# The delta rule's chunks of 128 tokens instead of 64, with the state products of one batch between the inverse levels of the next

## The reference

```python
def gated_delta_chunked(q, k, v, g, beta, s0):
    # S_t = a_t (I - b_t k_t k_t^T) S_{t-1} + b_t k_t v_t^T, o_t = S_t^T q_t
    g = jnp.cumsum(g, axis=-1)
    decay = jnp.exp(jnp.where(incl, g[..., :, None] - g[..., None, :], -jnp.inf))
    m = jnp.where(strict, jnp.einsum('bhnid,bhnjd->bhnij', k_beta, k) * decay, 0.0)
    t_inv = lax.linalg.triangular_solve(m + eye, ...)
    u = einsum(t_inv, v * beta)
    w = einsum(t_inv, k_beta * jnp.exp(g))
    def chunk_step(s, xs):
        v_new = u_c - w_c @ s
        o_c = q_c @ s + qk_c @ v_new
        s = s * a_c + k_c^T @ v_new
    ...
o = forward(q, k, v, s_fwd) + flip(backward(...))
```

## Time and profile before

| | us |
|---|---|
| median of 3 runs | 3282.56 (3279.77 to 3286.65) |
| profiled execution: span from first to last instruction | 3284.9 |
| TensorE busy | 2999.6 (91% of the span) |
| VectorE, ScalarE, GpSimd busy | 1235.7, 648.4, 250.2 |
| first block of `delta_net` | 11.85 |
| second block of `delta_net` | 491.7 |

### The profile page before, as it was taken

How to read it: one execution, slowest core, us unless ns; L and a number is a source line. 1 busy time by engine, 2 the same in 40 slices (tenths; PEclk the granted TensorE clock), 3 DMA queues, 4 the chain that set the end, 5 groups by cost and what they waited for, 6 DMA issues and landing times. The chain is left out here.

```text
span 3284.9 us, 43635 instructions
## 1 busy us (share of the span) xinstructions
PE 2999.6 (91%) x18685; PEld 1772.0 (54%) x18685; DVE 1235.7 (38%) x2364; ACT 648.4 (20%) x1444; POOL 250.2 (8%) x347
## 2 busy tenths in 40 slices
PE   6999998999898899999999979799999799999998
PEld 3434663456675555568888864366444444444443
DVE  1052451384443399425555546643001401111111
ACT  2111331011332355122112111532000100000000
POOL 0000110000010000013333310100000000000000
PEclk9999998998879899999999989899999799999999
DMA  7431013240001411000000021301321279999998
GB/s 259 153 133 46 1 52 97 89 78 27 1 1 65 152 52 51 12 29 3 2 2 2 2 88 69 115 1 68 146 76 51 88 322 427 427 427 426 427 427 361
DMA packets 130593, 431.68 MB, mean 131 GB/s; under 512 B 28978, under 2 KB 40502, under 8 KB 102621
## 3 DMA queue, kind: packets, MB, share of 16 engines
q1 hardware_dynamic: 130402, 428.89, 33.7%
HBM read 418.21 MB, written 10.66 MB: 131 GB/s over the span
## 5 line engine op out<-in xcount | busy, mean ns | idle before, releaser
L333 PE MATMUL banks<-weight_ring,rows_turned 128*128 128x512 f32 (+1 forms) x1576 | 679.7, 592 | 34.5 <-DMA weight_ring<-in_w_in 16.6
L333 PEld LDWEIGHTS banks<-weight_ring,rows_turned 128*128 128x128 f32 x1576 | 300.2, 196 | 406.7 <-issue 391.5
L2411 PE MATMUL banks<-rows_turned,weight_ring 128*128 128x256 f32 (+1 forms) x768 | 253.5, 490 | 1.8 <-PEq L1364 1.5
L2411 PEld LDWEIGHTS banks<-rows_turned,weight_ring 128*128 128x128 f32 x768 | 147.6, 192 | 101.0 <-issue 85.9
L3664 PE MATMUL banks<-weight_ring,chosen_turned 128*64 128x512 f32 (+1 forms) x696 | 174.3, 558 | 10.0 <-DMA weight_ring<-in_w_up 6.5
L3664 PE MATMUL banks<-expert_weights_early,chosen_turned 128*64 128x512 f32 (+1 forms) x672 | 169.3, 558 | 11.0 <-DMA expert_weights_early<-in_w_up 7.4
L1432 PE MATMUL banks<-weight_ring,mix_turned 128*128 128x512 f32 x320 | 138.8, 594 | 3.9 <-DMA weight_ring<-in_l_w_out 2.2
L3766 DVE TENSOR_TENSOR hidden<-hidden,banks 128x512 f32<-128x512 f32 (+1 forms) x24 | 14.0, 638 | 324.4 <-PE banks L3664 324.4
L2684 PE MATMUL banks<-v_channels 64*64 64x64 f32 (+1 forms) x2880 | 120.6, 231 | 0.7
L2684 PE MATMUL banks<-weight_ring 64*64 64x64 f32 (+1 forms) x2880 | 115.7, 226 | 0.4
L3664 PEld LDWEIGHTS banks<-weight_ring,chosen_turned 128*64 128x64 f32 x696 | 62.5, 137 | 97.4 <-issue 93.8
(11 more groups left out here) (550 smaller groups left out, 4378.3 us busy)
## 6 DMA issues: line engine op xcount, KB each, us to landing
weight_ring<-in_w_gate SPq DMA_DIRECT2D x29, 1408.0 KB, 17.6
weight_ring<-in_w_up SPq DMA_DIRECT2D x29, 1408.0 KB, 15.1
expert_weights_early<-in_w_gate SPq DMA_DIRECT2D x28, 1408.0 KB, 18.9
expert_weights_early<-in_w_up SPq DMA_DIRECT2D x28, 1408.0 KB, 15.6
expert_weights_early<-in_w_down SPq DMA_DIRECT2D x36, 1024.0 KB, 17.3
weight_ring<-in_w_down SPq DMA_DIRECT2D x35, 1024.0 KB, 17.4
weight_ring<-in_l_w_in SPq DMA_DIRECT2D x15, 2048.0 KB, 8.5
weight_ring<-in_w_in SPq DMA_DIRECT2D x13, 2048.0 KB, 7.8
```

The costliest lines, as they stand in the source:

```text
L333: ins = kit.nc.tensor.matmul(self.bank(u), lhsT, rhs, start=(k == 0), stop=(k == nk - 1))
L2411: ins = nc.tensor.matmul(kit.ps[:, bank(u), 0:n], w[:, k, f * P:(f + 1) * P], hT[:, k, h0:h0 + n], start=(k == 0), stop=(k == KD - 1))
```

## The change

A chunk is now a whole tile of 128 tokens. There are no u and w: the state is multiplied with the keys (`seen`), VectorE forms the residual `beta v - beta exp(g) k S` (`residual`), and the inverse with its decays folded in (`solver`, 128x128) turns it into v_new (`solve`); then `outer` for the state and `output`, which adds queries times state and scores times v_new in PSUM. The inverse keeps its two diagonal 64-blocks by the same levels; the block off the diagonal is two more products (`off`, `cross`). The inverse of the two halves is held with halves swapped, so that `level` and one product of `update` use the two quadrants off the array's diagonal, and the other product of `update` the diagonal ones. Keys are turned to token rows once, in the preparation, in twelve more groups. The decay differences no longer come from a product: the rows of cumulative decays and of their exponentials are parked in DRAM, and SP loads them on all partitions for each batch, 256 KB a load. The decays are not in the matrix while it is inverted, before or after.

The constants (line 1241) and the preparation:

```diff
     for d, before in (("f", col < row), ("b", col > row)):
-        incl = same & (before | (row == col))
-        parts["tri_" + d] = (incl.T) * 1.0
-        parts["tri_half_" + d] = own_half((incl.T) * 1.0)
-        parts["decay_t_" + d] = own_half(np.where(incl.T, 0.0, -NEG))
+        seen = (before | (row == col)).T
+        parts["tri_" + d] = (same & seen) * 1.0
+        parts["unseen_" + d] = np.where(seen, 0.0, -NEG)
     parts["same"] = same * 1.0
-    parts["half0"] = (row < CHUNK) * np.ones((1, P))
-    parts["half1"] = (row >= CHUNK) * np.ones((1, P))
+    parts["other"] = (~same) * 1.0
...
+        groups = list(v_groups)
+        for t in range(TA):
+            for h0 in (0, 4):
+                groups.append(([qk[:, 8 + h, at(t):at(t) + P] for h in range(h0, h0 + 4)], k_tok[:, t, h0 * P:(h0 + 4) * P].rearrange("p (h d) -> p h d", h=4)))
+        G = len(groups)
...
-            for i in range(8):
+            for i in range(10):
                 turn_v(pe, i)
             pe.wait_ge(asked.sem, asked(2))
...
-            for b, name in ((1, "same"), (2, "half0"), (3, "half1")):
-                ins = nc.tensor.matmul(kit.ps[:, b, 0:W], kit.part(name), flat(g), start=True, stop=True)
-            ins.then_inc(summed.sem, 1)
-            for i in range(8, G):
+            nc.tensor.matmul(kit.ps[:, 1, 0:W], kit.part("same"), flat(g), start=True, stop=True)
+            nc.tensor.matmul(kit.ps[:, 1, W:2 * W], kit.part("other"), flat(g), start=True, stop=True)
+            pe.wait_ge(given.sem, given(1))
+            nc.tensor.matmul(kit.ps[:, 0, W:2 * W], kit.part("swap_pairs"), flat(beta), start=True, stop=True).then_inc(summed.sem, 1)
+            for i in range(10, 17):
+                turn_v(pe, i)
+            pe.wait_ge(given.sem, given(3))
+            nc.tensor.transpose(kit.ps[0:W, 2, 0:P], flat(own), kit.ident)
+            nc.tensor.transpose(kit.ps[0:W, 2, P:2 * P], flat(eg), kit.ident).then_inc(summed.sem, 1)
+            for i in range(17, G):
                 turn_v(pe, i)
```

The loads, the products of a level, and TensorE's order:

```diff
+        def sync_loads(sp):
+            sp.wait_ge(parked.sem, parked(32))
+            for b, (r, t) in enumerate(batches):
+                w = (r * TA + t) * H
...
+                        sp.wait_ge(c.solver_ready.sem, c.solver_ready(b))
+                    if outs(b):
+                        sp.wait_ge(c.scores_ready.sem, c.scores_ready(outs(b)))
+                    src = rows_park[0, w + 4 * c.hg:w + 4 * c.hg + 4, :].rearrange("h n -> (h n)")
+                    sp.dma_start(c.decay.rearrange("p h n -> p (h n)"), row_bc(src)).then_inc(c.rows_landed.sem, 16)
+                for c in chains:
+                    if with_out(b):
+                        if outs(b):
+                            sp.wait_ge(c.out_summed.sem, c.out_summed(outs(b)))
+                        src = rows_park[1, w + 4 * c.hg:w + 4 * c.hg + 4, :].rearrange("h n -> (h n)")
+                        sp.dma_start(c.queries.rearrange("p h n -> p (h n)"), row_bc(src)).then_inc(c.queries_landed.sem, 16)
...
+            def level(c, b, i):
...
+                mask = c.odd if i % 2 else c.even
+                for h in range(4):
+                    for o_rows, other in (HALVES, HALVES[::-1]):
...
+            def update(c, b, i):
+                pe.wait_ge(c.z_ready.sem, c.z_ready(6 * b + i + 1))
+                pe.wait_ge(c.inverse_ready.sem, c.inverse_ready(6 * b + i + 1))
+                if b and i == 0:
+                    pe.wait_ge(c.solver_ready.sem, c.solver_ready(b))
+                first, later = in_order(batches[b][0])
+                for h in range(4):
+                    for o_rows, other in (HALVES, HALVES[::-1]):
+                        turned = nc.tensor.matmul(c.low(0)[other, h, :], c.inverse[o_rows, h, :], c.z[o_rows, h, :], start=True, stop=True, tile_position=(o_rows.start, other.start))
+                    for o_rows in HALVES if i < 4 else (later,):
+                        ins = nc.tensor.matmul(c.low(1)[o_rows, h, :], c.z[o_rows, h, :], c.inverse[o_rows, h, :], start=True, stop=True, tile_position=(o_rows.start, o_rows.start))
+                turned.then_inc(c.dt_summed.sem, 1)
+                ins.then_inc(c.d_summed.sem, 1)
...
+            left, right = chains
+            for it in range(N + 1):
...
+                stating = it > 0
+                for c in chains:
+                    keys(c, it)
+                for i in range(5):
+                    for c in chains:
+                        level(c, it, i)
+                    if stating and i == 0:
+                        seen(left, it - 1)
+                    if stating and i == 2:
+                        solve(right, it - 1)
+                    if stating and i == 3:
+                        outer(left, it - 1)
+                    if stating and i == 4:
+                        outer(right, it - 1)
+                    for c in chains:
+                        update(c, it, i)
+                    if stating and i == 0:
+                        seen(right, it - 1)
+                    if stating and i == 1:
+                        solve(left, it - 1)
+                    if stating and i == 2:
+                        output(left, it - 1)
+                    if stating and i == 3:
+                        output(right, it - 1)
+                for c in chains:
+                    off(c, it)
+                scores(left, it)
+                for c in chains:
+                    cross(c, it)
+                scores(right, it)
```

GpSimd's order and VectorE's; `mask` is a masked level, `base`, `shift`, `values`, `rest_keys` and `queries` are each one or two tensor_tensor operations:

```diff
+            for b in range(N):
+                for i in range(3):
+                    for c in chains:
+                        mask(c, b, i)
+                if b + 1 < N:
+                    for c in chains:
+                        base(c, b + 1)
+                shift(chains[0], b)
+                for c in chains:
+                    mask(c, b, 3)
+                shift(chains[1], b)
+                for c in chains:
+                    mask(c, b, 4)
+                for c in chains:
+                    values(c, b)
+                for c in chains:
+                    rest_keys(c, b)
+                for c in chains:
+                    queries(c, b)
...
+            def matrix(c, b):
+                dve.wait_ge(c.keys_summed.sem, c.keys_summed(b + 1))
+                nc.vector.tensor_tensor(c.matrix, c.high(0), per_row(c, beta, b, CHUNK), ALU.mult).then_inc(c.turned_ready.sem, 1)
+                if b:
+                    dve.wait_ge(c.solver_ready.sem, c.solver_ready(b))
+                dve.wait_ge(c.base_ready.sem, c.base_ready(b + 1))
+                step(dve, nc.vector.tensor_tensor(c.turned, c.high(0), c.base_mask, ALU.mult))
+                nc.vector.tensor_tensor(c.turned, c.turned, over_heads("ident_half"), ALU.add).then_inc(c.turned_ready.sem, 1)
+
+            def inverse_base(c, b):
+                name = f"level_{'fb'[batches[b][0]]}1"
+                dve.wait_ge(c.turned_ready.sem, c.turned_ready(7 * b + 1))
+                for o_rows, other in (HALVES, HALVES[::-1]):
+                    ins = nc.vector.tensor_tensor(c.inverse[other], c.matrix[o_rows], over_heads(name, o_rows), ALU.mult)
+                step(dve, ins)
+                nc.vector.scalar_tensor_tensor(c.inverse, c.inverse, -1.0, over_heads("ident_half"), ALU.mult, ALU.add).then_inc(c.inverse_ready.sem, 1)
...
+            def solver_own(c, b):
...
+                for o_rows in HALVES:
+                    nc.vector.tensor_tensor(c.solver[o_rows, :, o_rows], c.turned[o_rows], c.decay[o_rows, :, o_rows], ALU.mult)
+
+            def solver_off(c, b):
+                first, later = in_order(batches[b][0])
+                dve.wait_ge(c.d_summed.sem, c.d_summed(6 * b + 6))
+                nc.vector.scalar_tensor_tensor(c.solver[first, :, later], c.low(1)[first], -1.0, c.decay[first, :, later], ALU.mult, ALU.mult).then_inc(c.solver_ready.sem, 1)
...
+            def residual(c, s):
...
+                dve.wait_ge(c.values_ready.sem, c.values_ready(s + 1))
+                for h in range(4):
+                    ins = nc.vector.scalar_tensor_tensor(c.values[:, h, :], c.full(3)[:, h, :], beg[:, r, t, 4 * c.hg + h:4 * c.hg + h + 1], c.values[:, h, :], ALU.mult, ALU.add)
+                ins.then_inc(c.residual_ready.sem, 1)
...
+            for it in range(N + 1):
+                inverting, stating = it < N, it > 0
+                if inverting:
+                    for c in chains:
+                        matrix(c, it)
+                    for c in chains:
+                        inverse_base(c, it)
+                for i in range(5):
+                    if inverting:
+                        for c in chains:
+                            turned_update(c, it, i)
+                    if inverting and i < 4:
+                        for c in chains:
+                            inverse_update(c, it, i)
+                    if stating and i < 2:
+                        residual(chains[i], it - 1)
```

(12 more changed lines are left out.)

606 lines of the change are left out of this document (332 added, 274 removed).

## The result

The changed kernel takes 3194.62 us, median of 4 (3191.98 to 3198.46), beside 3284.61 us of the kernel before (3279.77 to 3287.48): a ratio of 0.9729, interval 0.9715 to 0.9742. It is 90.0 us faster; I had forecast 40 and a range that ends at 3195, 0.4 us above the result. The sign was right, the size less than half.

The account below looks back on a forecast made before the run. VectorE's work at the boundary between two inverses was taken to bound latent iterations. Chain stage -47.4 us and preparation +8.2, row loads at nothing, give -39.2; 3284.9 - 39.2 - 2.3 = 3243 us, range 3195 to 3280.

Parts of the forecast that it names:

- What bounds the kernel, and where the gain lies: VectorE's work around the boundary between two inverses bounds latent iterations; TensorE alone would save 12 us a batch; 56%.
- Opening, 8.2 us with collision: Start of an iteration on VectorE: two-input operations beside GpSimd take 0.83 instead of 0.42 us, 8.2 us for both chains.
- Updates of a pair at 1.9 us in levels 1 to 4: TensorE's update products of both chains in an inverse level take 1.9 us, from 29 ns a row.
- Wait for the second residual, 0.5 us in level 2: In level 2 TensorE waits from 15.5 to 16.0 us for VectorE's residual of chain 1.
- Clock, 1.0 us an iteration on top: Allowance of 1.0 us an iteration for a lower granted clock, as the new opening has waits of the same length.
- Rival (c): Waits in the opening drop the clock to 1.2 GHz into level 1: 60 us in all, 3303 us, slower than before; 9%.
- Tail, 6.6 us on VectorE: End of a latent iteration, 31.0 to 37.6 us, on VectorE; TensorE's 6 us of off-diagonal products, scores and keys fit beneath.
- Other iterations: Iterations besides forward latent ones: backward 40.1 us, context on context 33.5, context under latent 34.9, across passes 34.1, first 26.
- Preparation, 20 us: The stage's preparation grows from 11.85 to 20 us by twelve more turned groups: +8.2, between 5 and 11.
- Rows from DRAM at nothing: Four 256 KB row loads per latent batch stay hidden and cost nothing; row loads among the waits would mean wrong at root.
- Rival (d): Twenty changes of tile shape on TensorE cost 0.34 rather than 0.17 us each, 3.3 us an iteration: about 3283 us; 5%.
- rival (b): Four quadrants really work at once in the updates, 0.95 us a pair less in levels 1 to 3: 3201 us; 12%.

Follow-up runs that it names:

- Experiment 2: The changed kernel with GpSimd waiting ahead of the second level's masks until VectorE has both chains' inverse base: 3161.79 us, ratio 0.9628.
- experiment 1: The changed kernel with update products reordered so two quadrants alternate: crossing products before diagonal 3197.91 us, quadrants on the same rows 3224.62, on the same columns 3212.48.
- experiment 5: The changed kernel with the second chain's last state product at the end of the fourth level, where VectorE updates both states: 3188.39 us, ratio 0.9716.
- experiment 7: The changed kernel with the preparation's small products issued behind 8 turned groups of values instead of 10: 3192.11 us, preparation 19.44 instead of 22.84 us.
- experiment 6: The changed kernel with each load of decay and query rows issued twice, the second behind the first's landing: 3201.52 us, ratio 0.9747.
- experiment 3: The changed kernel with the second chain's product of keys and state issued ahead of the first level's two updates instead of behind them: 3177.29 us, ratio 0.9675.

## Why the prediction was wrong, step by step

- **What bounds the kernel, and where the gain lies**: right. A TensorE-only sum would have given 12 us a latent batch; the boundary on VectorE held it to 9.9 (44.16 to 34.26), though the updates were faster than in that sum. Experiment 2 shows it.
- **Opening, 8.2 us with collision**: 7.8 measured. Price of a two-input operation 0.72 to 0.85 where 0.83 was taken. The sum of 8.2 counted all eight at 0.83, although its words left the first out; with it left out it would have been 7.9.
- **Updates of a pair at 1.9 us in levels 1 to 4: the step that failed.** It rested on 29 ns a row. 17 ns a row makes 1.10 us. In the latent iteration, from its start: end of level 1 forecast 14.4, measured 14.4; level 2, 21.1 against 19.8; level 3, 27.2 against 25.0; level 4, 31.0 against 28.3; end 37.6 against 34.3. Level 1 alone shows no gain, because its state product of 2.07 us ran at the low clock and took it back.
- **The argument behind it**: I read 67 ns a row of the w product as the time of a weight load, one after another for the whole array, and halved it. Rows of different quadrants, their loads included, do go at the same time: 60 ns in one quadrant, 32 in two, 17 in four. The Trainium skill, TensorEngine Tiling (Array Packing), Key Properties, says that different tiles load weights and multiply in parallel; the rows of 17 ns agree, and at 12% I gave it too little.
- **Wait for the second residual, 0.5 us in level 2**: gone. VectorE had it at 1600.06, just as TensorE came to it (1600.12).
- **Clock, 1.0 us an iteration on top**: not needed as a term of its own in the walked iteration. Its cost is there, inside the measured 14.4 of level 1 (0.9 us on one state product alone), where the updates' gain paid for it. Rival (c), slower than before, had the fall right and its price wrong. In the walked iteration the clock fell for 3.4 us and came back; over the stage it was low for some 79 us, which can hold back at most 40 us of issue where (c) had 60, at the 0.90 that the prediction gave as (c)'s bound. And some 35 of the 79 us lie inside openings, where VectorE is the bound and a slow TensorE costs nothing (experiment 1). What the clock costs the changed kernel in all was not measured.
- **Tail, 6.6 us on VectorE**: 6.35. "TensorE's 6 us fit beneath" is right to 0.3 us, which experiment 5 found out.
- **Other iterations**: backward 40.1 against 35.7 to 36.7; context on context 33.5 against 28.5 and 30.2; context state under a latent inverse 34.9 against 31.2 and 29.7; across the passes 34.1 against 32.2; the first 26 against 24.2. Most miss by 3 to 5 us, the first and the one across the passes by 2.
- **Preparation, 20 us**: 22.84, the upper end of the 5 to 11 us that I gave it; the wait for the five small products was 2.69 us, not 1.2, and the clock 0.78 (experiment 7). The forecast was 2.8 us too low, and experiment 7 gets 1.4 to 3.7 us back.
- **Rows from DRAM at nothing**: GpSimd's waits for them, 16.9 us in four, stand at the queries' product and show no delay of TensorE; experiment 6 leaves 0 to 3 us open. The prediction gave row loads among the waits as a sign of being wrong at the root. They are among GpSimd's waits, so as it stands that sign came up; it should have named TensorE's and VectorE's waits.
- **Rival (d)**, changes of shape at 0.34 us: no. From the last update row ahead of the solve in level 1 (1597.69) to the first level product behind it (1598.92) are 1.23 us; its 8 rows at their pace of 0.112 us are 0.90, which leaves 0.17 us for each of the two changes, as taken.

Put together against the span: 3284.9 - 47.4 - 42 (the 3.5 us of rival (b) in 12 iterations) + 11.0 = 3206.5, and the profile has 3194.0. Of the 12.5 us left, 6.9 lie outside the function and 5.6 in the chain stage: forecast 444.3, with rival (b) 402.3, measured 396.7. But rival (b) counted 0.95 us a pair, and 0.8 were measured, so the updates explain some 35 of the 47.6 us by which the chain stage was missed (42 x 0.8 / 0.95, an estimate). The other 12 or so are smaller terms that were all taken too high: the openings (0.4 us each, some 5 in all), the wait of level 2 (up to 0.5 each), the last state (7.8 us for 9.5), and the clock's allowance of 12 us, only partly used. How these share the rest was not measured one by one.

## What to carry to other kernels

Where small products share an array, count how many quadrants a stretch keeps busy, and price a row by the pace of one quadrant divided by that number: here 60 ns, divided by one, two or four. Work around a boundary is best read as one chain: what delays an engine there on purpose (GpSimd by 3 us) can save more than it costs, since a two-input VectorE operation took twice as long beside it in the opening, and up to 3.4 times (1.43 us for 0.42) beside one long GpSimd product. And fill a wait of TensorE with work that has to be done anyway: in experiment 3 it paid once for the work and once for the clock. Last, when two orders of the same work differ in time, look where each one's slow stretches fall before you credit the order.

## What the hardware showed that I had not expected

- Rows of a later stretch started between those of an earlier one when they went to other quadrants: ten rows of line 2769, two of line 2772, three of 2769 again. So the starts of rows for different quadrants do not keep to the order of the program; the ends are modelled in the profile and tell nothing here.
- The slow stretch of the compared latent iteration, 3.4 us long, falls at 3.2, 7.7 or 9.3 us from its start, or in none of it, by small changes of order; other iterations have 6.8 or 10.2 us. Three kernels with equal pairs of updates differ by up to 27 us; in the iteration that I compared, its place accounts for 1.3 of 1.65 us. A slow stretch inside the opening cost nothing: 34.75 us with it, 34.76 without.
- The clock fell behind an opening in which TensorE was busy 3.73 of 7.90 us, and did not behind one with 4.57 of 7.80 (experiment 3). But this is no rule to go by: openings with 4.02 and 4.03 of 7.90 us busy, in the same iteration of two kernels, were followed by a slow stretch on the same rows and by none on the same columns (experiment 1).
